# A one-layer decoder block with 32 experts: expert weights loaded in 2 MiB slots with 16 KiB runs, gates and mixer projections computed transposed

## The reference, cut to what matters

```python
def reference(x, ...):                       # x (1, 256, 1024), all float32
    xn = rmsnorm(x, norm_mix_g)
    q_sb, k_sb, v_sb, q_mb, k_mb, v_mb, g_sb, g_mb = split(xn @ w_in)   # w_in 1024 x 5120
    y_sb = stick_breaking_attention(q_sb, k_sb, v_sb)                    # 8 heads of 64
    y_mb = moba_attention(q_mb, k_mb, v_mb, rel_bias)                    # 8 heads of 64, one block of 256
    merged = sigmoid(g_sb) * (y_sb @ w_proj_sb) + sigmoid(g_mb) * (y_mb @ w_proj_moba)
    h = x + merged @ w_out
    hn = rmsnorm(h, norm_ffn_g)
    gates = softmax over the top 4 of (hn @ w_router + b_router)         # 32 experts
    for e in range(32):                      # every expert: w_gate_up 1024 x 2048, w_down 1024 x 1024
        hgu = hn @ w_gate_up[e] + b_gate_up[e]
        gate, up = min(hgu[:, :1024], 7), clip(hgu[:, 1024:], -7, 7)
        y = ((up + 1) * gate * sigmoid(1.702 * gate)) @ w_down[e] + b_down[e]
        h += gates[:, e] * y
    return rmsnorm(h, norm_final_g)
```

## Time and profile before

| | |
|---|---|
| median of three runs | 1210.49 us (1210.0 to 1213.23) |
| the profiled execution: its own time / its span | 1212.92 / 1211.0 us |
| mean granted TensorE clock | 0.989 |
| busy: PE, DVE, ACT, POOL | 91%, 17%, 13%, 2% of the span |
| HBM read | 435.76 MB, 361 GB/s over the span |
| gate/up loads / down loads | 256 and 128 DMAs of 1024 KB |

### The profile page before, as it was taken

The page is one execution under the profiler, slowest core; times in us unless marked ns, Lnnn a source line. Parts: engine busy times, 40 slices in busy tenths (PEclk is TensorE's granted clock), DMA queues, the critical chain, the costliest instruction groups (busy, mean ns, idle before and its releaser), DMA issues.

```text
span 1211.0 us, 15516 instructions
## 1 busy us (share of the span) xinstructions
PE 1106.1 (91%) x6058; PEld 435.8 (36%) x6058; DVE 199.9 (17%) x418; ACT 156.1 (13%) x325; POOL 29.4 (2%) x73
## 2 busy tenths in 40 slices
PE   7999999989999999999988889999999999999985
PEld 6676444533333332232222323323323322322221
DVE  1311213231111111111111111111111111111111
ACT  2243230320000000000000000000000000000002
POOL 1010000200000000000000000000000000000000
PEclk9999999979999999999999999999999999999998
DMA  9923223289999999999999999999999999999994
GB/s 331 387 96 139 116 106 142 91 353 370 417 418 418 418 417 418 418 418 418 418 418 417 418 418 418 418 418 418 418 418 418 418 418 418 418 418 418 418 418 195
DMA packets 86724, 437.12 MB, mean 361 GB/s; under 512 B 7800, under 2 KB 7856, under 8 KB 53840
## 3 DMA queue, kind: packets, MB, share of 16 engines
q1 hardware_dynamic: 84880, 434.19, 88.3%
q10 hardware_dynamic: 1520, 1.59, 0.5%
q0 software_dynamic: 304, 1.06, 0.2%
HBM read 435.76 MB, written 1.06 MB: 361 GB/s over the span
## 4 chain that ended last, share of the span: by engine, by line
PE 40%; SPq 38%; DMA 17%; issue 3%; DVE 1%; ACT 0%; DVEq 0%; POOL 0%; POOLq 0%
SPq L319 20%; SPq L314 17%; DMA ring<-in_w_gate_up_dram 15%; PE bank L1160 14%; PE bank L946 7%; PE bank L943 5%; PE bank L1190 3%; PE bank L1143 2%; PE bank L1043 2%; PE bank L1057 2%; DMA ring<-in_w_down_dram 2%; PE bank L1179 1%; PE bank L1134 1%; PE bank L923 0%; PE bank L1173 0%
## 5 line engine op out<-in xcount | busy, mean ns | idle before, releaser
L1160 PE MATMUL bank<-ring,gates 128*64 128x512 f32 x2048 | 477.0, 604 | 18.3 <-DMA ring<-in_w_gate_up_dram 15.3
L1190 PE MATMUL bank<-ring,gates 128*64 128x512 f32 x1024 | 244.1, 603 | 59.8 <-DMA ring<-in_w_down_dram 59.8
L1160 PEld LDWEIGHTS bank<-ring,gates 128*64 128x64 f32 x2048 | 135.1, 137 | 277.2 <-issue 191.6
L849 DVE TENSOR_SCALAR gates<-bank 128x512 f32<-128x512 f32 x32 | 22.1, 692 | 786.5 <-PE bank L1160 786.5
L1190 PEld LDWEIGHTS bank<-ring,gates 128*64 128x64 f32 x1024 | 63.9, 136 | 238.5 <-DMA ring<-in_w_down_dram 152.2
L946 PE MATMUL bank<-ring,colsT 128*128 128x512 f32 x192 | 84.0, 594 | 0.0
L1143 PE MATMUL bank<-gates,scatter_w 64*128 64x512 f32 x256 | 63.6, 615 | 0.8 <-ACT gates L634 0.7
L943 PE MATMUL bank<-colsT,ring 128*128 128x256 f32 x256 | 57.3, 384 | 0.0
L630 ACT ACTIVATE gates<-gates 128x512 f32<-128x512 f32 x32 | 20.1, 630 | 277.1 <-DVE gates L849 277.1
L1134 PEld LDWEIGHTS bank<-onehot,qkT 128*128 128x128 bf16 x1488 | 45.1, 98 | 25.2 <-issue 25.2
L634 ACT ACTIVATE gates<-bank 128x512 f32<-128x512 f32 x32 | 19.1, 597 | 260.6 <-PE bank L1190 260.6
(11 more groups left out here) (167 smaller groups left out, 471.5 us busy)
## 6 DMA issues: line engine op xcount, KB each, us to landing
ring<-in_w_gate_up_dram SPq DMA_DIRECT2D x256, 1024.0 KB, 20.4
ring<-in_w_down_dram SPq DMA_DIRECT2D x128, 1024.0 KB, 24.4
ring<-in_w_in_dram SPq DMA_DIRECT2D x10, 2048.0 KB, 19.1
ring<-in_w_out_dram SPq DMA_DIRECT2D x1, 4096.0 KB, 13.9
ring<-in_w_proj_sb_dram SPq DMA_DIRECT2D x1, 2048.0 KB, 7.5
ring<-in_w_proj_moba_dram SPq DMA_DIRECT2D x1, 2048.0 KB, 7.6
resid<-in_x_dram SPq DMA_DIRECT2D x2, 512.0 KB, 3.6
bias<-u_scratch POOLq DMA_DIRECT2D x1, 1024.0 KB, 12.1
```

Source lines behind the costliest of these rows:

```text
L849: V.tensor_scalar(gate_t, bank[4][:, :], SWIGLU_LIMIT, None, ALU.min).then_inc(gate_rd, 1)
L1160: ins = mm(bank[4 + i][SLOTS * c:SLOTS * (c + 1), :], xeT[:, k, :], ring[:, k, i * D + c * CH:i * D + (c + 1) * CH], start=False, stop=k = ...
L1190: ins = mm(bank[6][SLOTS * c:SLOTS * (c + 1), :], rows, ring[:, KD + s, j * D + c * CH:j * D + (c + 1) * CH], start=k == 0, stop=k == KD - 1)
```

## The change: larger slots, longer runs, transposed gates and projections

- A slot holds 2 MiB, and `ring` has 6: slots 0 to 3 for w_gate_up (`GU` = 4), 4 and 5 for w_down. Partition p of gate/up slot s has the rows 256s+2p and 256s+2p+1, which lie next to each other in HBM: one run of 16 KiB. Partition p of down slot s has the four rows 512s+4p to 512s+4p+3, also one run of 16 KiB. There are 6 DMAs of 2 MiB for an expert where there were 12.
- The slices k of the contraction follow: `gather` takes every second column of `pieces` as stationary operand (a step of 2 bf16 elements), `hidden_columns` every fourth column of `h_t` (a step of 16 bytes), and the norm gain for `take` is loaded once more in this order (`gslot`, a DMA of 512 runs of 8 bytes on ScalarE's queue ahead of `gfin`).
- A slot is waited for before its first slice and counted as used behind its last one: two slices for gate/up, four for down.
- The gates are computed by sixteen "T" units instead of eight "N" units, four for each of the pairs 4 to 7, and lie transposed in the same buffer (`gatesT`).
- The mixer projections are computed transposed: 16 units of 4 slices x 256 columns instead of 8 of 4 x 512. VectorE's product and sum give `colsT` directly. The 16 transposes, their copies on VectorE and ScalarE, and VectorE's copy that only counted are gone. The last pair's `mix_values` stands behind unit 1 instead of unit 0.

```diff
-    RING = 12
-    SLOT = 2 * D
+    RING = 6
+    GU = 4
+    SLOT = 4 * D
...
+    fills = [[("T", c, j) for c in (Q_MB, K_MB) for j in range(4)][2 * p:2 * p + 2] for p in range(4)]
+    fills += [[("T", c, j) for j in range(4)] for c in range(6, NCH)]
+    fills[1].append(("N", V_MB, 0))
+    fills[3].append(("N", V_MB, 1))
+    fill_at = []
+    for more in fills:
+        fill_at.append(range(len(units), len(units) + len(more)))
+        units += more
...
+        gslot = sb("gslot", [P, KD // 2, 2])
...
+        gatesT = gates[:, :, :].rearrange("p t d -> p (t d)").rearrange("p (g n) -> p g n", n=T)
...
-            gu = w_gate_up[0].rearrange("e (k p) n -> e k p n", p=P)
-            dn = w_down[0].rearrange("e (k c p) n -> e k p c n", p=P, c=2)
+            gu = w_gate_up[0].rearrange("e (s p r) n -> e s p (r n)", p=P, r=2)
+            dn = w_down[0].rearrange("e (s p r) n -> e s p (r n)", p=P, r=4)
...
-                if s < KD:
-                    src = gu[e, s] if isinstance(e, int) else gu[bass.ds(e, 1), s].rearrange("o p n -> p (o n)")
-                    sp.dma_start(ring[:, s, :], src).then_inc(slot_in[s], 16)
-                else:
-                    dst = ring[:, s, :].rearrange("p (c n) -> p c n", c=2)
-                    src = (dn[e, s - KD] if isinstance(e, int)
-                           else dn[bass.ds(e, 1), s - KD].rearrange("o p c n -> p (o c) n"))
-                    sp.dma_start(dst, src).then_inc(slot_in[s], 16)
-
-
-            for s in (4, 5, 6, 7):
...
+            for s in (2, 3):
+                if s == 2:
                     sp.wait_ge(unit_ps, LAST_UNIT[9] + 1)
                 load_slot(0, s)
-            sp.wait_ge(out_ps, 8)
-            for s in (8, 9, 10, 11):
+            sp.wait_ge(out_ps, 2 * KD)
+            for s in (4, 5):
                 load_slot(0, s)
-            sp.wait_ge(out_ps, 12)
-            for s in (0, 1, 2, 3):
+            sp.wait_ge(out_ps, 2 * KD + 4)
+            for s in (0, 1):
                 load_slot(0, s)
 
-            def load_gate_up(e, done, first=0):
...
-                for k in range(first, KD):
-                    sp.wait_ge(gu_used, (e + done) * KD + (k + 1 - KD))
-                    load_slot(e, k)
+            def load_gate_up(e, done):
+                for s in range(GU):
+                    sp.wait_ge(gu_used, (e + done) * GU + (s + 1 - GU))
+                    load_slot(e, s)
...
+            with nc.allow_non_contiguous_dma(reason="two gains in a run"):
+                act.dma_start(gslot[:, :, :], norm_ffn_g[0].rearrange("(s p r) -> p s r", p=P, r=2)
+                              ).then_inc(late_in, 16)
...
-            for t in range(NT):
-                nc.scalar.activation(gates[:, t, :], gates[:, t, :], ACT.Sigmoid).then_inc(sigm_rd, 1)
+            for m in range(2):
+                nc.scalar.activation(gates[:, m, :], gates[:, m, :], ACT.Sigmoid).then_inc(sigm_rd, 1)
...
-            columns(1, 4, None)
...
-            dve.wait_ge(sigm_rd, NT)
             for m in range(2):
-                for t in range(NT):
-                    for c in range(2):
-                        n = 4 * m + 2 * t + c
-                        dve.wait_ge(out_ps, n + 1)
-                        g = gates[:, t, m * D + c * CH:m * D + (c + 1) * CH]
-                        link(V.tensor_tensor(g, g, bank[n % 4][:, :], ALU.mult))
-                        if m == 0:
-                            V.tensor_copy(stat[:, 60:61], stat[:, 6:7]).then_inc(merged, 1)
-                        else:
-                            V.tensor_tensor(scaled[:, t, c * CH:(c + 1) * CH], gates[:, t, c * CH:(c + 1) * CH], g,
-                                            ALU.add).then_inc(merged, 1)
-            columns(1, 4, None)
+                dve.wait_ge(sigm_rd, m + 1)
+                for j in range(KD):
+                    n = KD * m + j
+                    dve.wait_ge(out_ps, n + 1)
+                    g = gatesT[:, n, :]
+                    if m == 0:
+                        V.tensor_tensor(g, g, bank[n % 4][:, 0:T], ALU.mult).then_inc(merged, 1)
+                    else:
+                        link(V.tensor_tensor(g, g, bank[n % 4][:, 0:T], ALU.mult))
+                        V.tensor_tensor(colsT[:, j, :], gatesT[:, j, :], g, ALU.add).then_inc(merged, 1)
             def add_rows(n):
...
                 pe.wait_ge(pv_rd, 4 * (m + 1))
-                for t in range(NT):
-                    for c in range(2):
-                        n = 4 * m + 2 * t + c
-                        if n == 0:
-                            pe.wait_ge(unit_rd, NU)
-                        if n >= 4:
-                            pe.wait_ge(merged, n - 3)
-                        for k in range(4):
-                            ins = mm(bank[n % 4][:, :], yT[:, 4 * m + k, t * P:(t + 1) * P],
-                                     w[:, k, c * CH:(c + 1) * CH], start=k == 0, stop=k == 3)
-                        ins.then_inc(out_ps, 1)
-                        if n == 0:
-                            mix_values(PAIRS - 1)
-            pe.wait_ge(merged, 8)
-            transposes(4)
+                for j in range(KD):
+                    n = KD * m + j
+                    if n == 0:
+                        pe.wait_ge(unit_rd, NU)
+                    if n >= 4:
+                        pe.wait_ge(merged, n - 3)
+                    for k in range(4):
+                        ins = mm(bank[n % 4][:, 0:T], w[:, k, j * P:(j + 1) * P], yT[:, 4 * m + k, :], start=k == 0,
+                                 stop=k == 3)
+                    ins.then_inc(out_ps, 1)
+                    if n == 1:
+                        mix_values(PAIRS - 1)
             pe.wait_ge(wout_in, 16)
 
             def out_rows(n, ks):
                 t, c = divmod(n, 2)
                 for k in ks:
                     if n == 0:
-                        column(1, k)
+                        pe.wait_ge(merged, max(2 * KD - 3, KD + k + 1))
...
-                            ins = mm(bank[7][:, k * SLOTS:(k + 1) * SLOTS], pieces[i][:, t, k * P:(k + 1) * P],
+                            ins = mm(bank[7][:, k * SLOTS:(k + 1) * SLOTS], pieces[i][:, t, 2 * P * (k // 2) + k % 2:2 * P * (k // 2 + 1):2],
...
-                    pe.wait_ge(slot_in[k], g * 16 + 16)
+                    if k % 2 == 0:
+                        pe.wait_ge(slot_in[k // 2], g * 16 + 16)
                     for i in range(2):
                         for c in range(2):
+                            n0 = (k % 2) * 2 * D + i * D + c * CH
                             ins = mm(bank[4 + i][SLOTS * c:SLOTS * (c + 1), :], xeT[:, k, :],
-                                     ring[:, k, i * D + c * CH:i * D + (c + 1) * CH], start=False,
-                                     stop=k == KD - 1)
-                    ins.then_inc(gu_used, 1)
+                                     ring[:, k // 2, n0:n0 + CH], start=False, stop=k == KD - 1)
+                    if k % 2 == 1:
+                        ins.then_inc(gu_used, 1)
 
             def scatter_rows(g):
...
-                    ins = tp(bank[7][:, c * P:(c + 1) * P], h_t[:, c * P:(c + 1) * P], ident[:, :])
+                    ins = tp(bank[7][:, c * P:(c + 1) * P], h_t[:, c::4], ident[:, :])
...
-                for s in range(RING - KD):
-                    pe.wait_ge(slot_in[KD + s], g * 16 + 16)
-                    for j in range(2):
-                        k = 2 * s + j
-                        rows = hT[:, k % 4, SLOTS * (k // 4):SLOTS * (k // 4) + SLOTS]
+                for s in range(RING - GU):
+                    pe.wait_ge(slot_in[GU + s], g * 16 + 16)
+                    for j in range(4):
+                        k = 4 * s + j
+                        rows = hT[:, j, SLOTS * s:SLOTS * s + SLOTS]
                         for c in range(2):
```

More of the change, by code:

```diff
@@ L74, in hybrid_layer @@
     lead = len(units)
-    first_fill = [("T", Q_MB, j) for j in range(4)] + [("T", K_MB, j) for j in range(4)]
-    first_fill += [("N", c, t) for c in range(6, NCH) for t in range(NT)]
-    second_fill = {3: ("N", V_MB, 0), 6: ("N", V_MB, 1)}
-    fill_at, second_at = {}, {}
-    for p in range(NH // 2):
-        for s in (2 * p, 2 * p + 1):
-            fill_at[s] = len(units)
-            units.append(first_fill[s])
-        for s in (2 * p, 2 * p + 1):
-            if s in second_fill:
-                second_at[s] = len(units)
-                units.append(second_fill[s])
+    fills = [[("T", c, j) for c in (Q_MB, K_MB) for j in range(4)][2 * p:2 * p + 2] for p in range(4)]
[6 more added lines that the diff above has]
+        units += more
     unit_no = {u: n for n, u in enumerate(units)}
@@ L322, in _ @@
-            for s in (4, 5, 6, 7):
-                if s == 4:
+                src = gu if s < GU else dn
+                q = s if s < GU else s - GU
+                piece = src[e, q] if isinstance(e, int) else src[bass.ds(e, 1), q].rearrange("o p n -> p (o n)")
```

(27 more changed lines are left out.)

29 lines of the change are left out of this document (11 added, 18 removed).

## The result

The changed kernel takes 1197.74 us (median of four runs, 1196.81 to 1198.70). The ratio is 0.9885, with a 95% interval of 0.9869 to 0.9900: 1.15% faster, 14.1 us. The profiled execution took 1196.85 us, with a span of 1195.0 us. The forecast was 1193 us, faster; its sum was -17.05 us between two profiled executions, and these differ by 16.0 us of span.

What follows compares the result with a forecast made beforehand. For about 75% of the span the weight stream (bytes divided by rate) was taken to bound the kernel. Stream -19.8, last start +0.75 and tail +2.0 gave -17.05 us, forecast 1193 us, range 1179 to 1208.

Steps and rivals of the forecast that it cites:

- the last start: Weight stream's final restart after its pause near 275 us: forecast at 277.25 us, 0.75 us late.
- the stream: The 364 MiB of expert weights loaded after the last start: forecast to take 19.8 us less.
- the tail: Last expert's down weights: a gap of up to 0.75 us and 1.25 us more matmul work, together 2.0 us lost.
- The price of a MiB: Load time per MiB of expert weights: forecast to fall from 2.5165 to 2.462 us (426 GB/s) with 16 KiB runs.
- Rivals 1 (8 KiB is enough): Weight stream: 16 KiB runs no faster than 8 KiB, only down gains; 4.35 us gained, 1206 us; chance 0.13.
- 2 (418 is a ceiling): Weight stream: path limited to 418 GB/s whatever the runs; 1213 us, no change that can be told; chance 0.09.
- 4 (long runs are worse): Weight stream: long runs suit HBM worse, 2.545 us per MiB, 10.4 us more; 1224 us; chance 0.05.
- rival 5: Weight stream: rate reaches 433 GB/s (2.42 us per MiB), 35.1 us saved; 1178 us; chance 0.05.
- rival 3: Expert loop: strided gather loads no longer overlap, gather takes 6.8 us, TensorE 31.1 us per expert; 1256 us; chance 0.06.
- The head: TensorE's work before the experts: pairs +1.1, mixer +0.7, removed wait before the output projection -3.45; sum -1.65 us.
- the sentence on `gslot`: ScalarE's queue gets gslot ahead of gfin; VectorE waits for it, but idles 15.71 us beforehand, which hides it.
- TensorE's room: Expert loop: TensorE's 25.86 us per expert leaves 3.7 us below the new 29.5 us load time; gather losses fit inside.

Runs made afterwards that it cites:

- e4: Changed kernel with the same 2 MiB DMAs but every run 8 KiB, without gslot: 1206.82 us, 0.9948 to the kernel before.
- e3: Changed kernel with 2 MiB DMAs but the old runs (8 KiB gate/up, 4 KiB down), without gslot: 1215.85 us, 1.0029 to the kernel before.
- e2: Kernel before with the transposed gates and mixer projections alone (1 MiB slots, old runs, no gslot): 1207.82 us, 0.9970 to the kernel before.
- e8: The changed kernel itself, unchanged, measured once more beside the others: 1197.32 us, 0.9872 to the kernel before.
- e1: Changed kernel with the loads gslot and gfin moved from ScalarE to SyncE behind w_out: 1191.36 us, 0.9826 to the kernel before.
- e9: Changed kernel with gslot alone moved from ScalarE to SyncE behind w_out, gfin left on ScalarE: 1194.53 us, 0.9847 to the kernel before.
- e6: Changed kernel with the changes of e1 and e5 together: 1187.63 us, 0.9798 to the kernel before.
- e5: Changed kernel with the last expert's down weights loaded into gate/up slots 0 and 1: 1192.85 us, 0.9840 to the kernel before.

## Why the prediction was right, point by point

In the terms of the sum, the last start came out at 0 (+0.75 forecast), the stream at -19 (-19.8) and the tail at +3 (+2.0): -16.0 between the two profiled executions, against -17.05. Of the 4.7 us between 1193 and the measured 1197.74, 1.35 are the fourth run of the kernel before, which moved its median from 1210.49 to 1211.84.

**The price of a MiB** carried it, and was a little too careful: 2.462 us forecast, 2.447 measured. The second step, 6 ns a run, was read from two short stretches, 412 and 420 GB/s. Over 470 us e4 shows 422 for 8 KiB, which with the 418 of the mix leaves 410 for 4 KiB: 9 ns a run there too. The argument (a fixed price per run, 6 to 10 ns on each engine, read from three sizes) holds; e3 and e4 give 9 ns and show that the size of the DMA has no part in it. With 364 MiB the rate alone gives 364 x (2.5165 - 2.447) = 25.3 us, but the stream took only 19 us less: some 6 us went into pauses, about 1 of it from 276 to 280 us (279 GB/s) and 5 from 1158 us on (82 GB/s from 1158 to 1161). The sentence "Behind this start there is no gap" was wrong, and the tail's gap was put at up to 0.75. So the term of -19.8 came out as -19 by two errors that cancel, and that is luck. Rivals 1 (8 KiB is enough), 2 (418 is a ceiling) and 4 (long runs are worse) are refuted by e3, e4 and the plateau, and rival 5 (433 GB/s) by the plateau. Two slips in rival 3 change nothing: 6.8 - 1.57 is 5.2, not 5.26, and 4.27/48 us and 33 ns make 122 ns, not 121.

**The head**, forecast at -1.65 us, was +1.3 to +1.5. The pairs cost less than said (4 x (14.08 - 14.00) = 0.3 us, not 1.1: in a row of four, units take 0.220 us an instruction). Mixer and merge together gave 3.3 us where 3.45 - 0.7 = 2.75 were forecast: from the start of the mixer's last block to the output projection it was 27.61 us (179.84 to 207.45) and is 24.28 (184.66 to 208.94). So without `gslot` the head would have been at -3.0, as in e2. The step that failed is the sentence on `gslot`: I asked who waits for its landing (VectorE, well covered) and not what its issue does to ScalarE, which has to copy units right behind it. Price: 4.5 us at the end of the lead in the first profile (58.94 against 54.46 before; 2.46 of it standing, 1.3 at the low clock) and 3.0 in e8's, where the clock did not fall. e1 and e9 get back all but 0.6 and 0.2 of it.

**The last start** was forecast at 277.25 and is at about 276.5, although the head is 3 us later than forecast. Two things made up for it: from the output projection to the first slice it took 61.87 us where it was 64.35, with a higher clock on the way (0.83 from 240 to 250 us, where it was 0.62), and the two slices took 4.75 us, not 6.00, since the clock rose earlier. This is no merit of the change: it is luck. The level of 1.2 GHz near 270 us comes for a different length from execution to execution. A stretch of e1, then of e6, which have the same head:

```profile
266.00:275.00 9.00, 9.00 (x25) 2.53 (x23) 2.82 (x6) 0.00 (x0) 0.00 (x0) 0.62 0.87 367
```

```profile
266.00:275.00 9.00, 9.00 (x42) 3.02 (x41) 1.76 (x5) 0.47 (x2) 0.00 (x0) 1.00 0.98 396
```

With a mean clock of 0.62 TensorE does 25 instructions in these 9 us, with 1.00 it does 42; e1's last start is near 276.5 us, e6's near 272.5. So up to 4 us of a single profile at this place is clock, and e1 against e6 cannot be read from one profile each. The times of all runs show it too. Of the 20 runs of the kernel before that stand beside e1 to e4, the seven with a mean clock of 0.992 or 0.993 took 1209.1 to 1211.0 us, the three with 0.991 1212.4 to 1213.6, and the ten with 0.989 1212.8 to 1214.1. e2 splits alike, 1206.7 to 1207.8 (0.992 to 0.994) and 1210.1 to 1211.5 (0.989): 3 us from level to level, and 3 us below the kernel before at either. So medians of five runs can differ by 3 us through this alone. What decides the level is not shown.

**The tail** was forecast at +2.0 (0.75 of pause and 1.25 of matmuls) and is 3 to 3.5 behind the stream, with the 5 us of pauses inside it. The mechanism was the one named (the reload waits for the same slot, and that is now four slices), but I let it act on the last slot alone; it also delays the first of the two, and the wait lowered the clock (5.17 instead of 3.65 us). e5 shows it.

**TensorE's room.** The gather lost nothing: 48 loads with a step of two elements still take 1.57 us, which refutes rival 3. The transposes of `h_t` did lose, as the step of 16 bytes let expect. Weight loads of both lines after, ns min/median/max:

```profile
L1119 PEld LDWEIGHTS bank<-onehot,qkT x1488: 96/98/101, 259.2 to 1122.5; 128*128 128x128 bf16 x186
L1166 PEld LDWEIGHTS bank<-ident,gates x128: 195/211/219, 279.4 to 1165.2; 128*128 128x128 f32 x128
```

98 ns as in the earlier trace rows; 211 ns where there were 141, 0.1 us more per expert on the timeline. The Trainium skill ("TensorE: Matmul & The Clock Gate", Weight-path perf modes) had said that a small column step costs bf16 weights nothing; the trace agrees, 98 ns and 98 ns.

e3 and e4 vary the step of `h_t`: adjacent columns, then a step of 8 bytes.

```profile
L1164 PEld LDWEIGHTS bank<-ident,gates x128: 137/141/144, 275.3 to 1184.7; 128*128 128x128 f32 x128
L1164 PEld LDWEIGHTS bank<-ident,gates x128: 194/209/219, 279.4 to 1178.1; 128*128 128x128 f32 x128
```

141 ns, 209 and, with 16 bytes, 211: it is the step that costs, and half the step costs the same. The Trainium skill ("SBUF — State Buffer", Specifications, Cachelines) says that full bandwidth needs at least two hits in each 16-byte line, and that each cross to a new line pays a penalty. A step of 8 bytes has two hits in each line and half as many lines as one of 16, and the trace has 209 ns against 211. So this rule, on which the prediction leaned for `h_t`, does not explain the 211; what does is open.

The prediction also held a fit of 2.0 us per DMA, from the Trainium skill ("DMA: Bandwidth & Descriptors"), against the trace. By it e3 would have gained, and e3 has no gain. The page gives this fit in its section "Anatomy of one DMA", not in "Bandwidth", and for DMAs issued from GpSimd; these loads are issued from SyncE.

## What to carry to other kernels

In a stretch that one stream of loads bounds, count runs, not DMAs: each contiguous piece of 4 to 16 KiB cost each engine the same 9 ns here, so fit the price from the sizes the trace already has. Larger slots allow longer runs, at a price where the stream starts and ends (e3 is 8 us above e2), so look there for waits on a slot that another free buffer could take. A small load with many short runs is not free because nobody waits for its data: ask what its issuer has to do next. And before a block of matmuls is moved out of the way, ask which engine used that time.

## What the runs showed that I had not expected

- 9 ns per run on each of 16 engines between 4 and 16 KiB, the same over both steps (418, 422, 428 GB/s).
- 512 runs of 8 bytes lengthen the issue of the next DMA on the same queue from 1.02 to 4.52 us, and the issuing engine stands for it.
- A float32 weight load of 128 x 128 takes 141 ns from adjacent columns, 209 with a step of 8 bytes and 211 with one of 16; a bf16 load takes 98 with and without a step of two elements.
- The same instructions near 270 us run at a mean clock of 0.62 or 1.00 in two kernels that are alike up to there, and shift all that follows by about 4 us; over many runs of one kernel the times fall into two groups 3 us apart.
